# Turning the output projection of a streaming encoder layer: weights held still, merged rows moving, and the final norm along the partitions

## What is computed

```python
p = rms_norm(x, norm_g) @ w_in                       # 1024 -> 5376 columns
aq, ak, av, ag, bq, bfg, bi, bg, ma, mb = split_projection(p)
...                                                  # window attention (a) and gated recurrence (b)
ya = (attn_o * jax.nn.silu(ag)) @ w_ba
yb = (rn.reshape(bsz, t, B_WIDTH).astype(x.dtype) * jax.nn.silu(bg)) @ w_bb
merged = jax.nn.sigmoid(ma) * ya + jax.nn.sigmoid(mb) * yb
return x + merged @ w_o                              # w_o is 1024 x 1024

y_prompt = rms_norm(hp, final_norm_gain)             # the final norm, over the 1024 of each row
y_sample = rms_norm(hs, final_norm_gain)
```

## Time and profile before

| | |
|---|---|
| median of 3 runs | 1603.62 us (1603.17 to 1603.66) |
| the profiled execution | 1606.24 us, of which the trace spans 1604.2 us |
| mean granted TensorE clock | 0.985 of 2.4 GHz |
| busy: TensorE / VectorE / ScalarE / GpSimd | 96% / 58% / 32% / 14% of the span |
| output stage of group 0, start to start of what follows | 506.65 to 578.55 us |

### The profile page before, as it was taken

One profiled execution on the slowest core, in us unless ns is written; L12 is line 12 of the kernel. 1 busy time (PEld: TensorE's weight loads), 2 busy tenths in 40 slices (PEclk: granted clock), 3 DMA queues, 4 the chain that ended last, 5 costly groups with the idle time before them and its releaser, 6 DMA issues.

```text
span 1604.2 us, 23628 instructions
## 1 busy us (share of the span) xinstructions
PE 1538.0 (96%) x9427; PEld 1433.4 (89%) x9427; DVE 927.8 (58%) x1471; ACT 512.9 (32%) x1114; POOL 224.2 (14%) x155
## 2 busy tenths in 40 slices
PE   7999999878899999999999999999999999999997
PEld 6998899778899789999999999879999999999975
DVE  5667877863367644567777136645467758414613
ACT  5355553433223222555223120212256423211002
POOL 1431224245444400000100000100000010000000
PEclk9999999988999999999999999999999999999998
DMA  4743344367787563222236885535322233886451
GB/s 154 282 158 129 125 150 160 122 237 278 265 320 271 194 242 139 106 89 102 86 108 220 273 287 201 178 130 204 127 92 101 91 109 109 260 275 213 133 189 72
DMA packets 95963, 279.94 MB, mean 175 GB/s; under 512 B 11888, under 2 KB 22896, under 8 KB 95856
## 3 DMA queue, kind: packets, MB, share of 16 engines
q1 hardware_dynamic: 70800, 204.25, 37.4%
q10 hardware_dynamic: 25056, 74.20, 11.9%
HBM read 195.57 MB, written 82.84 MB: 174 GB/s over the span
## 4 chain that ended last, share of the span: by engine, by line
PE 86%; DVE 9%; issue 2%; ACT 2%; DMA 1%; POOL 0%; ACTq 0%; DVEq 0%
PE bank L1273 22%; PE bank L1275 21%; PE bank L1274 21%; PE bank L1504 4%; PE bank L1505 4%; PE bank L1506 4%; PE bank L1475 2%; PE bank L1401 1%; PE bank L1419 1%; PE bank L1433 1%; PE bank L1471 1%; PE bank L1443 1%; PE bank L1457 1%; PE bank L1410 1%; DVE rs L1150 1%
## 5 line engine op out<-in xcount | busy, mean ns | idle before, releaser
L1273 PE MATMUL bank<-x_hi,w_unit 128*128 128x320 f32 (+2 forms) x1680 | 555.5, 331 | 34.0 <-ACT u_sum L869 27.5
L1275 PE MATMUL bank<-x_hi,w_unit 128*128 128x320 f32 (+2 forms) x1680 | 545.4, 325 | 0.0
L1274 PE MATMUL bank<-x_lo,w_unit 128*128 128x320 f32 (+2 forms) x1680 | 544.9, 324 | 0.0
L1273 PEld LDWEIGHTS bank<-x_hi,w_unit 128*128 128x128 f32 x1680 | 318.8, 190 | 45.7 <-issue 36.4
L1274 PEld LDWEIGHTS bank<-x_lo,w_unit 128*128 128x128 f32 x1680 | 319.1, 190 | 0.1
L1275 PEld LDWEIGHTS bank<-x_hi,w_unit 128*128 128x128 f32 x1680 | 318.6, 190 | 0.0
L591 POOL TENSOR_TENSOR w_unit<-w_raw,w_unit 128x512 fp32r<-128x512 f32 x102 | 142.3, 1414 | 309.2 <-ACT w_unit L646 283.3
L1504 PE MATMUL bank<-w_unit,m_hi 128*128 128x512 f32 (+1 forms) x288 | 116.2, 404 | 4.0 <-issue 3.8
L1505 PE MATMUL bank<-w_unit,m_hi 128*128 128x512 f32 (+1 forms) x288 | 113.7, 395 | 0.0
L1506 PE MATMUL bank<-w_unit,m_lo 128*128 128x512 f32 (+1 forms) x288 | 113.5, 394 | 0.0
L1255 DVE TENSOR_TENSOR res<-res,bank 128x512 f32<-128x512 f32 (+1 forms) x36 | 24.7, 685 | 114.0 <-PE bank L1506 114.0
(11 more groups left out here) (203 smaller groups left out, 2570.1 us busy)
## 6 DMA issues: line engine op xcount, KB each, us to landing
w_unit<-w_parts SPq DMA_DIRECT2D x274, 512.0 KB, 4.1
w_parts<-w_unit ACTq DMA_DIRECT2D x137, 512.0 KB, 4.0
w_raw<-in_w SPq DMA_DIRECT2D x88, 256.0 KB, 3.5
res<-in_x SPq DMA_DIRECT2D x15, 512.0 KB, 7.2
out_y<-res SPq DMA_DIRECT2D x15, 512.0 KB, 4.0
raw<-in_w SPq DMA_DIRECT2D x28, 256.0 KB, 4.3
x_raw<-in_x_t SPq DMA_DIRECT2D x12, 384.0 KB, 8.1
x_raw<-in_x_t SPq DMA_DIRECT2D x12, 320.0 KB, 5.7
```

Of the source, the lines that this page charges most:

```text
L1273: pe.matmul(out, w_h, m_h, start=first, stop=False, **more)
L1274: pe.matmul(out, w_h, m_l, start=False, stop=False, **more)
L1275: return pe.matmul(out, w_l, m_h, start=False, stop=last_of_bank, **more)
```

## The change

The output weights become the stationary side and the merged rows stream, 320 or 384 columns at a time, as in the projections: `out` is now the same code on TensorE as `proj`. A step `("out", a, s)` makes 128 output channels (block `wo{a}`) for half s in one bank, 24 matmuls, with no drain, and the 16 steps share 3 banks in rotation. Blocks 0 to 3 go with both halves each; blocks 4 to 7 first all with half 0, then all with half 1 (`OUT`).

`res` and y now have the model dimension on the partitions; the residual is read from the transposed x, and the host turns y back. The final norm's sum runs over partitions, so it takes the same way as x's: ScalarE squares each finished piece of `res` and multiplies it by the gain, VectorE adds the squares up in `y_acc`, one float32 matmul with ones per half sums them (`y_sum`), ScalarE takes the root, VectorE inverts it and multiplies 8 pieces (`y_back`). Half 0 gets its norm within the stage, before the last two `out` steps; half 1 gets it after the next group's `ak` and `av`, or at once in the last group. `x_split` is cut in two parts, and x's steps are spread over the new list.

The core of the diff (`sp` is SyncE, `act` ScalarE, `dve` VectorE, `pe` TensorE; in its last part `out` joins `proj` and the old `out` with its drain goes):

```diff
-X_STEPS = [("x_square", 0, 0), ("x_sum", 0, 0), ("x_square", 1, 0), ("x_split", 0, 0),
-           ("x_sum", 1, 0), ("x_split", 1, 0)]
-OUT_BANKS = [3, 4, 5, 0, 1, 2]
+X_STEPS = {0: [("x_square", 0, 0)], 2: [("x_sum", 0, 0)], 4: [("x_square", 1, 0), ("x_split", 0, 0)],
+           5: [("x_split", 0, 1)], 8: [("x_sum", 1, 0), ("x_split", 1, 0)], 9: [("x_split", 1, 1)]}
+OUT = ([(j, s) for j in range(KT // 2) for s in range(2)] + [(j, s) for s in range(2) for j in range(KT // 2, KT)])
+SQUARES = len(OUT) - 2
...
+    if g:
+        out[4:4] = [("y_sum", 1, g - 1)]
+        out[7:7] = [("y_back", 1, g - 1)]
...
-    for p in range(KT):
+    for n, (j, s) in enumerate(OUT):
         if not last:
-            out += {0: X_STEPS[:1], 1: X_STEPS[1:2], 2: X_STEPS[2:4], 4: X_STEPS[4:]}.get(p, [])
-        out.append(("out", p // 4, p % 4))
+            out += X_STEPS.get(n, [])
+        out.append(("out", j, s))
+        if (j, s) == (KT - 3, 1):
+            out += [("y_sum", 0, g), ("y_back", 0, g)]
+    if last:
+        out += [("y_sum", 1, g), ("y_back", 1, g)]
...
-                    for i, (t0, n) in enumerate(TILES):
-                        sp.dma_start(res[0:n, i, :], x[g, t0:t0 + n, :]).then_inc(res_in[i], 16)
+                    for q in range(4):
+                        k = slice(2 * q, 2 * q + 2)
+                        sp.dma_start(res[:, k, :], x_t[g, :, k, :]).then_inc(res_in[q], 16)
...
-                    ahead(f"wo{a}{s}")
+                    if s == 0:
+                        ahead(f"wo{a}")
...
+                    wait_read(act, g, last, step, bank)
...
+                    act.activation(y_acc[:, lo:hi] if n < 2 else y_sq[:, n % 2, 0:hi - lo], res[:, a, lo:hi],
+                                   ACT.Square).then_inc(y_squared, 1)
+                    act.activation(res[:, a, lo:hi], res[:, a, lo:hi], ACT.Copy,
+                                   scale=fgain[:, a:a + 1]).then_inc(y_scaled, 1)
...
+                    wait_full(dve, g, last, step, bank)
+                    dve.wait_ge(res_in[a // 2], 16 * (g + 1))
+                    dve.tensor_tensor(r, r, pb[bank][:, 0:hi - lo], ALU.add).then_inc(read[bank], 1)
+                    if n > 2:
+                        add_out_squares(g, n - 1)
...
+                elif kind == "y_back":
...
+                    link(dve.reciprocal(y_acc[:, lo:hi], y_acc[:, lo:hi]))
+                    dve.wait_ge(y_scaled, len(OUT) * (s + 1) - (0 if a else KT // 2))
+                    for k in range(KT):
+                        r = res[:, k, lo:hi]
+                        ins = dve.tensor_tensor(r, r, y_acc[:, lo:hi], ALU.mult)
...
-                if kind == "proj":
-                    b = BLOCK[a]
+                if kind in ("proj", "out"):
+                    b = BLOCK[a if kind == "proj" else f"wo{a}"]
...
-                    pe.drain().then_inc(piece_used, 1)
+                elif kind == "y_sum":
...
+                    pe.matmul(pb[b][:, 0:hi - lo], ones[:], y_acc[:, lo:hi], start=True, stop=True).then_inc(full[b], 1)
```

More of the change, by code:

```diff
@@ L57 @@
 BLOCKS = (PLAIN + MIXED + [f"wab{j}" for j in range(MERGES)]
-          + [f"wo{hf}{kp}" for hf in range(2) for kp in range(KT // 2)])
+          + [f"wo{j}" for j in range(MERGES)])
 NB, NP = len(BLOCKS), len(PLAIN)
@@ L405, in wait_used @@
         elif BLOCKS[name].startswith("wo"):
-            eng.wait_ge(piece_used, 8 * g + 4 * int(BLOCKS[name][2]) + int(BLOCKS[name][3]) + 1)
-            return
+            step = ("out", int(BLOCKS[name][2:]), 1)
         elif BLOCKS[name].startswith("wab"):
@@ L542, in body @@
                 load_block(g, b)
+                if g and b == HALVES // 2 + 1:
+                    store_y(g - 1, 1)
             if g == 0:
@@ L608, in body @@
                     x_back(t_top[:, 0], 0, 1)
-                if name == (BLOCK["wo03"], 1) and not last:
+                if name == (BLOCK["wo3"], 1) and not last:
                     add_squares(pool, 1, g + 1)
@@ L688, in prepare_x @@
             else:
-                for q in range(4):
+                for q in (2 * step[2], 2 * step[2] + 1):
                     k = slice(2 * q, 2 * q + 2)
@@ L699, in _ @@
         act.activation(root[:], eps[:], ACT.Sqrt)
-        for step in X_STEPS:
+        for step in X_ALL:
             prepare_x(step, None, 0, False)
@@ L917, in prepare_x @@
             elif kind == "x_split":
-                rms = x_acc[:, s, 1, 0:n]
-                wait_read(dve, g, last, ("x_sum", s, 0), 6 + s)
-                link(dve.reciprocal(rms, rms))
+                rms, part = x_acc[:, s, 1, 0:n], step[2]
+                if part == 0:
+                    wait_read(dve, g, last, ("x_sum", s, 0), 6 + s)
+                    link(dve.reciprocal(rms, rms))
                 def x_low(q):
@@ L928, in x_low @@
                                       ALU.subtract).then_inc(x_split, 1)
-                for q in range(4):
+                for q in (2 * part, 2 * part + 1):
                     for kt in (2 * q, 2 * q + 1):
@@ L937, in prepare_x @@
                         x_low(q - 1)
-                x_low(3)
+                if part:
+                    x_low(3)
         dve.memset(eps[:], EPS)
@@ L956, in _ @@
         dve.wait_ge(gain_in, 16)
-        for step in X_STEPS:
+        for step in X_ALL:
             prepare_x(step, None, 0, False)
-        dve.wait_ge(consts_in, 16 * 7)
+        dve.wait_ge(consts_in, 16 * 8)
         link(dve.tensor_scalar(neg_sink[:], sink[:], -1.0, None, ALU.mult))
@@ L1488, in body @@
                               start=False, stop=True).then_inc(full[b], 1)
[L1489 to L1510 removed]
+                elif kind == "y_sum":
+                    lo, hi = sub(a)
+                    b = banks(step)[0]
+                    pe.wait_ge(y_added, SQUARES * s + (SQUARES if a else SQUARES - 4))
+                    wait_bank_free(pe, g, last, step, b)
+                    pe.matmul(pb[b][:, 0:hi - lo], ones[:], y_acc[:, lo:hi], start=True, stop=True).then_inc(full[b], 1)
                 elif kind.startswith("x_"):
```

171 lines of the change are left out of this document (74 added, 97 removed).

## The result

The changed kernel takes 1594.66 us (median of 5 runs, 1592.15 to 1599.65), and the kernel before 1603.62 (1602.97 to 1605.47, 5 runs): a ratio of 0.9947 [0.9926, 0.9968]. Forecast was 1595.8. Run again in the last batch of experiments, the two kernels gave 0.9953 [0.9940, 0.9967]. So the change is worth some 8 us by the ratios. Forecast and median lie 1.1 us apart, and part of that is luck: single runs of the changed kernel spread over 7.5 us here, and its median in the last batch was 1598.11.

A forecast was written before the change was run, and what follows sets the result against it. TensorE was taken to bound the kernel (86% of the chain). Stage savings of 24.4 us, less 3.4 for the tail and 9.9 and 3.3 for waits, gave -7.8: 1603.6 becomes 1595.8 us, range 1584 to 1603.

The forecast's parts named there:

- Matmuls and sums: TensorE's output stages: cheaper matmuls, no piece-end gaps, less the added sums over partitions; 24.4 us saved before waits.
- 61.4 + 0.57: Group 2's output stage: 61.4 us of matmuls plus one sum over partitions of 320 columns, 62.0 in all.
- the estimate of the prediction: A line through the skill's matmul spacings: about 110 ns at 352 columns, so 4.6 us lost in each group.
- The sums over partitions: x's and y's sums on TensorE: 0.57 us for 320 columns, 0.68 for 384; 2.5 us in groups 0 and 1.
- The waits: TensorE waiting in the output stages for emptied banks and weights: 9.9 us in group 0, 3.3 in group 1.
- the walk: Engine lists followed through group 1's stage: scalings slowed beside GpSimd, step 4's bank emptied at 27.8, 3.3 us of wait.
- That clock: TensorE's clock falling after group 0's long wait: in step 10 only shortens the wait for `wo7`, so nothing added.
- the term for steps 7 and 8: Waits for VectorE to empty the banks of steps 4 and 5: 0.7 us at step 7, 1.8 in all.
- The residual: Its load, needed by step 3 at 11.8 us, is there by 9: no wait, 2 us of margin.
- The tail: From the last output matmul's end to the span's end: 14.8 us for 11.4, so 3.4 us more.
- the prediction's clock: Time in the tail counted with 0 at the last output matmul's end; VectorE ends half 0's norm at -0.5.
- The likeliest case: Waits as forecast and the price of matmuls right: 1590 to 1601 us; chance 0.52.

The follow-up runs named there:

- the run with weights and squares: Changed kernel with `wo6`'s and `wo7`'s high parts moved earlier on ScalarE and x's second squares at step 2, not 4: 1593.59 us, ratio 0.9927 to before.
- the fastest kernel: Changed kernel with `wo6`'s and `wo7`'s high parts ahead of x's second root and high parts, x's second squares at step 2: 1589.94 us.
- split late: Changed kernel with x's second sum and split moved before steps 11 and 12 in place of 8 and 9: 1596.04 us, ratio 0.9961 to before.
- weights first: Changed kernel with `wo6`'s high part before x's second root and `wo7`'s before x's second pair of high parts, on ScalarE alone: 1594.60 us.
- `wo7` before x: Changed kernel with `wo6`'s high part before x's second root and `wo7`'s ahead of x's first pair of high parts: 1594.31 us.

## Why the prediction was right, point by point

**Matmuls and sums.** Group 2's stage of 61.98 us is the 61.4 + 0.57 of the prediction, and the stages without waits in the run with weights and squares (63.2 in group 1) are its 61.4 + 1.8. Without waits the three stages would be 25.9 us shorter than before, and the two sums of half 1 take 1.3 of that back between them: 24.6 us for the 24.4 of the forecast. Its parts stand too: 3.7, 3.7 and 3.3 us a group are the drain's, measured alone, for a forecast of 3.5, and the rest the columns'.

The Trainium skill's spacings (TensorE: Matmul & The Clock Gate, Back-to-back issue gap) would, by the estimate of the prediction, have made the new form slower by 4.6 us a group. The trace disagrees: without its drain the old form takes 67.0 us in group 2, the new one 61.98 with a sum that the old one doesn't have.

**The sums over partitions.** `y_sum` moved the next matmul by 0.54 us for 320 columns (forecast 0.57), and by 0.64 for 384 (forecast 0.68).

**The waits** were forecast at 9.9 and 3.3 us and cost 11.4 and 2.4: 13.8 for 13.2, from errors of both signs. In group 1 VectorE did what the walk gave: four scalings took 6.74 us beside GpSimd, and the emptying of step 4's bank began 27.4 us from the stage's start (forecast 27.3). Step 7 cost 0.9 us for 0.7, step 8 0.3 for 1.1, and step 12 1.1 for 1.5. In group 0 the forecast had 1.8 us at steps 7 and 8, 4.9 for `wo6` and 3.2 for `wo7`; measured are 3.0, 4.9, and 3.4 with the slow clock of step 10. That clock did shorten the wait for `wo7`, as argued: 2.2 us of the 3.4 are the clock, 1.2 the wait. What was too small is the term for steps 7 and 8, taken over from group 1: in group 0 GpSimd makes a low part at that time, an addition of VectorE took 1.23 us beside it for 0.55, and the next two scalings 2.05 for 1.00. The residual was no wait, as forecast: its first part landed 6.1 us into the stage. `ak` did not wait for its weights either.

**The tail** was 14.9 for 14.8, by errors that cancel. ScalarE loads a table before half 0's root (1.28 us; the prediction has none), which brings the end of half 0's norm on VectorE from -0.5 to +0.3 on the prediction's clock. In the rows each multiplication starts some 0.07 us before the one ahead of it ends, so VectorE's instructions, too, are priced from start to start. The sum of half 1 with ones takes 1.6 us to its root, not 0.9: it comes after a wait of 2.77 us, at a granted clock of 0.56, and its matmuls take 1.52. (When the changed kernel was run again they took 0.91 behind the same wait, and the tail was 14.3.) Against that, multiplications in a row take 0.41 and 0.48 us each and not 0.49 and 0.56, 1.3 us less over both halves.

**The sum.** -24.6 + 3.5 + 13.8 = -7.3 by the measured terms, for a forecast of -7.8. With the wait of 0.67 us between the stages, which the prediction doesn't have, that is within 0.1 of the -6.7 that the profile shows outside the part ahead of the first stage. The medians show -9.0 and, in the last batch, -5.8 (1598.11 for 1603.95). The likeliest case was the right one, and by its own mechanism.

**What was not argued.** The prediction counted 5.9 us a group for the columns and 3.5 for the drains and drew nothing from the second number: the drains could go without turning anything round. Measured, that alone gives 0.9936 [0.9924, 0.9948]. Of the 24.6 us of the change, 10.7 are the drains'; the other 13.9 are more than eaten by waits and tail, 17.3 us. Only with its waits cut does the turned-round form seem to get ahead: the fastest kernel has 0.9911 [0.9897, 0.9925], and the old form without drains 0.9936 [0.9924, 0.9948], from another batch; the intervals just touch.

**Contention.** The Trainium skill's rule (GPSIMD Engine Reference, Specifications: GpSimd shares its SBUF interfaces with VectorE, with contention for VectorE instructions that have two SBUF inputs) agrees with the runs: with GpSimd's additions moved away most of the cost at steps 7 and 8 goes, and the inverse, which has one input, kept its 2.15 us. But the claim for the waits of group 0 needed more: there ScalarE's list, VectorE's list and the landing of `wo7` lie within 2 us of one another. Taking away one showed the next, three times (split late, weights first, `wo7` before x). Each alone brought the stage of 74.6 us to between 72.1 and 73.6; with the contention gone as well it fell to 68.8, and 5.6 us over the 63.2 without waits are left. Whether they can go too was not tried.

## What to carry to other kernels

Before you change the shape of a product to save columns, take out what stands between the products and measure that by itself: here one instruction in 24 places was worth as much as the whole change. A stage with no wait in it has slack in its other engines that a profile doesn't print; when a new form makes each step wait for a bank, walk the lists of all engines and price every wait, since here more than half of the saving on TensorE went there. And compare two kernels by their stages and by medians of several runs, not by the spans of two profiles.

## What the runs showed of the hardware

- A drain on TensorE costs 0.44 to 0.47 us (0.44 by a piece of before, 3.7/8 and 3.3/7 taken out, 6.8/15 put in), whether the matmuls around it have 512, 384 or 320 columns.
- On VectorE four scalings of 128x320 took 3.02 us when they ran beside a little work of GpSimd and 6.74 beside its additions of three 128x768 pieces; the inverse of 128x320 took 2.14 to 2.15 us either way. An addition of 128x320 took 1.85 in place of 0.48. One scaling that began 0.36 us into a GpSimd addition of 2.14 us ended 0.36 us after it, and one that began 0.11 us before it took its 0.55.
- ScalarE loaded a table for 1.28 us before the first root of the last stage, at 1570.69.
- A wait that TensorE's rows show as 0.65 us costs 0.92 from start to start.
